# Stage boundaries of a two-layer decoder kernel, with the last two and the next four weight items done for one half of the sequence and then for the other

## The reference

```
c_act = silu(c)
for i in (0, 1):
    sh_m, sc_m, g_m, sh_f, sc_f, g_f = split(c_act @ mod_w[i] + mod_b[i], 6)
    h = modulate(rmsnorm(x, norm_mix_g[i]), sh_m, sc_m)
    y = gla_mixer(h, ...) if i == 0 else mla_attention(h, ..., shared_kv)
    x = x + (1 + g_m) * y
    h = modulate(rmsnorm(x, norm_ffn_g[i]), sh_f, sc_f)
    x = x + (1 + g_f) * conv_ffn(h, ...)      # up (2048 -> 2*5632), conv, silu, down
return rmsnorm(x, final_norm_g)
```

## Time and profile before

| | |
|---|---|
| Median of three runs | 2383.03 us (2381.65 to 2386.59) |
| The profiled execution, its own time | 2379.23 us |
| Its span | 2377.1 us |
| TensorE busy | 2301.8 us (97%) |
| VectorE busy | 1849.8 us (78%) |
| ScalarE busy | 1096.3 us (46%) |
| Mean granted TensorE clock | 0.986 |
| HBM over the span | 266 GB/s |

### The profile page before, as it was taken

The page is one execution under the profiler, slowest core; times in us unless marked ns, Lnnn a source line. Parts: engine busy times, 40 slices in busy tenths (PEclk is TensorE's granted clock), DMA queues, the critical chain, the costliest instruction groups (busy, mean ns, idle before and its releaser), DMA issues.

```text
span 2377.1 us, 26862 instructions
## 1 busy us (share of the span) xinstructions
PE 2301.8 (97%) x10800; PEld 1865.5 (78%) x10800; DVE 1849.8 (78%) x1766; ACT 1096.3 (46%) x1192; POOL 111.3 (5%) x127
## 2 busy tenths in 40 slices
PE   5999999999999999999998999999999999999997
PEld 2478887788887888878886888778887888878886
DVE  5868997888997898889898777787787556564565
ACT  2244443444554354533554545434654345544453
POOL 0021740000000000000000000000000000000000
PEclk8999999999999999999999999999999999999999
DMA  9957789788987998889888375785776555555554
GB/s 362 385 201 287 256 298 354 271 305 299 339 327 271 350 342 306 291 327 378 313 285 325 120 238 184 274 327 215 280 282 213 193 182 191 177 186 192 187 182 154
DMA packets 259807, 632.89 MB, mean 266 GB/s; under 512 B 23505, under 2 KB 32745, under 8 KB 233978
## 3 DMA queue, kind: packets, MB, share of 16 engines
q1 hardware_dynamic: 258050, 625.90, 74.1%
q10 hardware_dynamic: 1656, 5.60, 0.6%
HBM read 629.36 MB, written 2.10 MB: 266 GB/s over the span
## 4 chain that ended last, share of the span: by engine, by line
PE 49%; issue 34%; DVE 8%; DMA 5%; ACT 2%; SPq 1%; POOL 0%; POOLq 0%; DVEq 0%; ACTq 0%
PE gm L1960 12%; PE gm L1961 12%; PE gm L1967 12%; DVE acc L1242 2%; PE tp L2003 2%; DVE w_lo L1225 2%; DMA mods<-in_mod_w_dram 1%; PE gm L1952 1%; ACT w_hi L763 1%; PE gm L1954 1%; PE gm L1953 1%; PE ms L2113 1%; DMA raw<-in_ffn_w_down_dram 1%; PE ms L2247 1%; DMA raw<-in_mla_w_o_dram 1%
## 5 line engine op out<-in xcount | busy, mean ns | idle before, releaser
L1225 DVE TENSOR_TENSOR w_lo<-raw,w_hi 128x2048 fp32r<-128x2048 f32 (+1 forms) x378 | 851.9, 2255 | 325.3 <-ACT w_hi L763 323.6
L763 ACT ACTIVATE w_hi<-raw 128x2048 fp32r<-128x2048 f32 (+1 forms) x378 | 703.8, 1864 | 697.2 <-DMA raw<-in_ffn_w_up_dram 241.7
L1960 PE MATMUL gm<-w_hi,h_hi 128*128 128x512 f32 x1816 | 720.6, 397 | 1.7 <-DVE h_lo L1353 1.6
L1961 PE MATMUL gm<-w_hi,h_lo 128*128 128x512 f32 x1816 | 708.1, 390 | 0.0
L1967 PE MATMUL gm<-w_lo,h_hi 128*128 128x512 f32 x1816 | 448.7, 389 | 0.0
L1242 DVE SCALAR_TENSOR_TENSOR acc<-mods,c_col,acc 128x2048 f32<-128x2048 f32 x180 | 422.7, 2348 | 5.4 <-DMA mods<-in_mod_w_dram 4.2
L1960 PEld LDWEIGHTS gm<-w_hi,h_hi 128*128 128x128 f32 x1816 | 341.1, 188 | 78.0 <-issue 4.4
L1967 PEld LDWEIGHTS gm<-w_lo,h_hi 128*128 128x128 f32 x1816 | 340.8, 188 | 70.8
L1961 PEld LDWEIGHTS gm<-w_hi,h_lo 128*128 128x128 f32 x1816 | 341.3, 188 | 69.9 <-issue 1.7
L1960 PE MATMUL gm<-w_hi,a_hi 128*128 128x512 f32 x692 | 273.4, 395 | 11.1 <-DVE a_lo L1727 7.9
L1961 PE MATMUL gm<-w_hi,a_lo 128*128 128x512 f32 x692 | 269.6, 390 | 0.0
(11 more groups left out here) (275 smaller groups left out, 2137.5 us busy)
## 6 DMA issues: line engine op xcount, KB each, us to landing
raw<-in_ffn_w_up_dram SPq DMA_DIRECT2D x176, 1024.0 KB, 5.1
mods<-in_mod_w_dram SPq DMA_DIRECT2D x170, 1024.0 KB, 7.2
raw<-in_ffn_w_down_dram SPq DMA_DIRECT2D x64, 1024.0 KB, 5.1
raw<-in_gla_w_in_dram SPq DMA_DIRECT2D x48, 1024.0 KB, 5.2
mods<-in_kv_mod_w_dram SPq DMA_DIRECT2D x32, 1024.0 KB, 7.0
raw<-in_ffn_w_down_dram SPq DMA_DIRECT2D x32, 768.0 KB, 4.4
raw<-in_gla_w_o_dram SPq DMA_DIRECT2D x16, 1024.0 KB, 7.1
raw<-in_mla_w_o_dram SPq DMA_DIRECT2D x16, 1024.0 KB, 6.0
```

The source lines that it names most:

```text
L763: act.activation(w_hi[:, k % RAW, 0:words], raw[:, k % RAW, 0:words], ACT.Copy).then_inc(hi_made, 1)
L1225: dve.tensor_tensor(w_lo[:, k % RAW, 0:words], raw[:, k % RAW, 0:words], w_hi[:, k % RAW, 0:words].bitcast(F32), ALU.subtract).then_inc(lo ...
L1960: pe.matmul(o, hi_s[:, kt, tok], wh[:, j, :], start=kt == 0, stop=False)
L1961: pe.matmul(o, lo_s[:, kt, tok], wh[:, j, :], start=False, stop=False)
```

## The change

At each boundary the last two items of the stage and the first four of the next are done for t = 0 and then for t = 1. The normalised rows have a place per half: `x_tok[0]` over the second `mods` slot, `x_tok[1]` over `gate_b`. Fill f of a boundary is now four feature tiles of one token half: t = f // 4, tiles 4 (f % 4) to 4 (f % 4) + 3. Mean and power are made per half. The column sums come behind both last items, in two parts of eight columns. The first modulation load of `up00` and of `up10` waits for all eight fills. `add_last`, `boundary_root`, `normalise_chunks`, `first_split`, `reduced` and `late_normalise` go, the loops over items are otherwise as they were, `MOD_PLACES` too.

```diff
+    x_tok = (place("x_tok0", MD + 8192, [P, D], F32), place("x_tok1", GU, [P, D], F32))
...  # SP
+                elif n == first_mod("up00"):
+                    sp.wait_ge(tp_done, a["norm1"].tp + 8)
...  # ScalarE
+            def round_fill(name, f, dst):
+                act.wait_ge(both_made, 4 * BOUND[name] + f // 2 + 1)
+                act.activation(part(dst, f), both_v[:, :, :], ACT.Copy).then_inc(split_hi, 1)
+            def scale_fill(name, f, dst, scale, shift):
...
+                for j in range(4):        # 128 x 128 each, tp -> both_a
...
+                act.activation(part(dst, f), both_a[:, :, :], ACT.Copy).then_inc(split_hi, 1)
+            def turn_boundary(stage, name, nxt, dst, scale, shift, columns):
+                last_square(stage, name, 0)
+                normalise_rest(name, 0)       # 128 x 1536
+                last_square(stage, name, 1)
+                hi(nxt + 2)
+                round_fill(name, 0, dst)
+                act.wait_ge(columns_on, columns - (name != "norm2"))
+                scale_fill(name, 1, dst, scale, shift)
+                normalise_rest(name, 1)
+                round_fill(name, 2, dst)
+                act.wait_ge(columns_on, columns)
+                scale_fill(name, 3, dst, scale, shift)
+                hi(nxt + 3)
+                round_fill(name, 4, dst)
+                scale_fill(name, 5, dst, scale, shift)
+                round_fill(name, 6, dst)
+                scale_fill(name, 7, dst, scale, shift)
...  # VectorE
+            def add_half(stage, name, t):
+                if t == 0:
+                    dve.wait_ge(sq_made, 8 * BOUND[name] + 6)
...                    # the two sums of squares
+                    dve.wait_ge(half_used, BOUND[name] + 1)
...                    # product with the gate, sum into x, for t = 0
+                else:
+                    dve.wait_ge(item_used, a[stage].item + 16)
...                    # the same for t = 1
+                add_half(stage, name, 0)
+                mean_token(name, 0)
+                normalise_first(0)            # 128 x 512
+                lo(nxt + 1)
+                add_half(stage, name, 1)
+                mean_token(name, 1)
+                reduced_half(columns, 0)
+                scaled(0)                     # 4 of 128 x 128, tp -> both_v
+                low_part(0)
+                low_part(1)
+                normalise_first(1)
+                reduced_half(columns, 1)
+                scaled(2)
+                low_part(2)
+                lo(nxt + 2)
+                low_part(3)
+                scaled(4)
+                low_part(4)
+                lo(nxt + 3)
+                low_part(5)
+                scaled(6)
+                low_part(6)
+                low_part(7)
...  # TensorE
+            def last_items(stage, name, columns, specs, **how):
+                for t in range(TT):
+                    for i, spec in enumerate(specs):
+                        turns = t == 1 and i == 0 and name != "final"
+                        ins = token_item(t, *spec, middle=(lambda: token_fill(name, 0)) if turns else None, **how)
+                        if turns:
+                            token_fill(name, 1)
+                    if t == 0:
+                        ins.then_inc(half_used, 1)
+                if columns:
+                    reduce_mod(columns)
+            def first_items(name, first, fills, *src):
+                for t in range(TT):
+                    for k in range(4):
+                        f = 4 * t + k
+                        pe.wait_ge(tp_free, a[name].tp + f + 1)
+                        if f + 2 < fills:
+                            token_fill(name, f + 2)
+                        token_item(t, first + k, first + k, *src, 0, k)
```

More of the change, by code:

```diff
@@ L547, in load_item, with first_mod @@
                 sp.dma_start(dst, src).then_inc(raw_in[n % RAW], 16)
+            def first_mod(name):
+                return min(m[0] for item_, ms_ in mod_at.items() if item_ >= a[name].item for m in ms_)
             def load_mod(n, g, kt):
@@ L734, in _ @@
                 root(TT * h, TT, DV, o_sums, TT * (h + 1), o_rstd)
[L735 to L738, removed]
+            for name in ("norm1", "norm2"):
+                mean_root(name, 0)
+                mean_root(name, 1)
+            mean_root("norm3", 0, TT)
+            mean_root("norm4", 0, TT)
             pool.wait_ge(tp_free, at["norm4"].tp + 2)
@@ L828, in turn_boundary, with last_square @@
[L828 to L839, removed]
+            def last_square(stage, name, t):
+                if t == 0:
+                    act.wait_ge(x_half, BOUND[name] + 1)
+                else:
+                    act.wait_ge(x_added, added[stage] + 4)
+                chunk_squares(name, 3, t)
@@ L856, in turn_two @@
                 kv, mix = ab[:, A_OF["kv"]], ab[:, A_OF["mix1"]]
[L857 to L860, removed]
+                turn_boundary("down02", "norm2", next_item, a_hi, kv, ab[:, A_OF["kv"] + 1], COLUMNS_ON[9])
+                for f in range(8, 16):
+                    if f % 2:
                         hi(next_item + (f + 1) // 2)
@@ L2036, in reduce_mod @@
                 else:
[L2037 to L2041 removed]
+                    for half in range(2):
+                        o = ms_open(fill + half)
+                        for j in range(8):
+                            c0 = (8 * half + j) * P
+                            ins = pe.matmul(o[:, j:j + 1], acc[:, g % 2, c0:c0 + P], ones[:, 0:1],
+                                            start=True, stop=True)
+                        ins.then_inc(ms_done, 1)
             def reduce_turned(g, part):
@@ L2090, in body @@
                 def body(i, turned=None, last=False):
-                    for k in range(8):
+                    for k in range(8 - LAST[name] if last else 8):
                         if k % 4 == 0:
@@ L2094, in body @@
                         turn = turned if k < 4 else None
-                        item(s.item + 8 * i + k, s.item + k, hi_s, lo_s, k // 4, k % 4, turn=turn,
-                             halves=last and k == 7)
+                        item(s.item + 8 * i + k, s.item + k, hi_s, lo_s, k // 4, k % 4, turn=turn)
                         if turned and k >= 4:
@@ L2302, in _ @@
             section("gla_out", h_hi, h_lo, turn_o)
-            reduce_mod(4)
+            s = a["gla_out"]
+            last_items("gla_out", "norm1", 4, [(s.item + k, s.item + k, h_hi, h_lo, 1, k % 4) for k in range(16 - LAST["gla_out"], 16)])
             def turn_pair(layer, g, i, j):
@@ L2343, in ffn @@
                             gm_free(s.chunk + ch)
+                        if g == 2 and k >= 16 - LAST[name]:
+                            if k == 16 - LAST[name]:
+                                last_items(name, ("norm2", "final")[layer], (10, None)[layer],
+                                           [(s.item + n, s.item + n, a_hi, a_lo, 1, DOWN[2][n][1]) for n in range(k, 16)],
+                                           k_tiles=blocks, total=4 * blocks)
+                            continue
                         if ch == 0:
@@ L2359, in _ @@
             s, m = a["latent"], a["mla"]
-            reduce_mod(10)
-            for k in range(8):
-                if k % 4 == 0:
-                    gm_free(s.chunk + k // 4)
-                src = (a_hi, a_lo) if k < 4 else (h_hi, h_lo)
-                first = KT if k >= 4 else 0
-                item(s.item + k, s.item + k, *src, k // 4, k % 4,
-                     turn=lambda kt, first=first: turn_wide("norm2", first + kt, fills=16))
+            gm_free(s.chunk)
+            first_items("norm2", s.item, 16, a_hi, a_lo)
+            gm_free(s.chunk + 1)
+            for k in range(4, 8):
+                item(s.item + k, s.item + k, h_hi, h_lo, 1, k % 4,
+                     turn=lambda kt: turn_wide("norm2", KT + kt, x_tok, 16))
             def turn_latents(name, side):
```

397 lines of the change are left out of this document (193 added, 204 removed).

## The result

| | before | after |
|---|---|---|
| median of the runs (four each, on one chip) | 2383.60 us | 2405.53 us |
| lowest to highest | 2381.65 to 2386.59 | 2404.45 to 2410.68 |
| profiled execution: span | 2377.1 us | 2402.7 us |

The change makes the kernel slower: ratio 1.0092, 95% interval 1.0075 to 1.0108. The forecast was 2404 us.

A forecast was written before the change was run, and what follows sets the result against it. TensorE, busy 97%, bounds the kernel; at stage boundaries VectorE's backlog makes the sum late. Norm1 +9.0, norm5 +8.95, norm2 +8.1 and the end -2.5 sum to +23.5: 2402.7 or 2406.5 by base, stated 2404 us, range 2388 to 2413.

The forecast's parts named there:

- (a): Norm1, last two items: half 0 is signalled at 517.45, but busy VectorE starts its sum at 522.51, 5.06 us later.
- (b): Norm1, second pass: TensorE stands 7.7 us at fill 0's transposes, waiting for the normalised half 0; bounds 2.6 and 8.5.
- (c): Rest of norm1's second pass: low clock behind the wait, pass ends at 533.9, +11.0 us; 2.6 less at full rate.
- the rival of a clock that stays up: Boundaries: the 7.7 us of standing stay but 2.6 x 3 go, 2396 us; chance 0.08.
- (d): Norm1, pass's end to next stage's first matmul: half 1's chain takes 6.9 us against 8.62, -1.7; column sums cost nothing.
- (e): Next four items after norm1: one transpose group fewer, -0.5, low clock longer, +0.2, together -0.3 us; bound +1.7.
- (f): End of the kernel: half 0's output leaves early, last transfer issued at about 2369.5 instead of 2371.51; -2.5 us, bounds -1 and -4.
- (g): SP's load queue: weight slots come free later, but item 4 is there 1.6 us early; cost 0, bound +2.2 each.
- The rival on the other side: Boundaries: VectorE takes the half at its signal, stall 2.6 us with the clock up, -0.4 each, 2379.3 us; chance 0.07.

The follow-up runs named there:

- e5: Kernel of e2 with ScalarE's rounding of the next stage's second item also moved behind the normalisation of half 0: 2397.79 us, ratio 1.0070.
- e2: Changed kernel with VectorE's w_lo and, at norm1 and norm5, a modulation product moved behind half 0's normalisation; at norm2 two products go earlier: 2403.74 us, 1.0076.
- e6: Changed kernel with 26 further matmuls that nobody reads ahead of fill 0's transposes in the second pass: 2398.54 us, ratio 1.0061.
- e7: Changed kernel with column sums moved into the second pass's stall, and half 0's first two parts made ahead of the sum of half 1: 2383.16 us, 1.0003.
- e4: Kernel before with only the end as in the changed kernel, the three stage boundaries as before: 2380.26 us, ratio 0.9980.
- e10: Kernel before with the new end and the third group's item order in the down projections' first two groups: 2367.23 us, ratio 0.9915.
- e11: Kernel before, unchanged, profiled a second time: 2380.85 us, span 2379.0.
- e12: Changed kernel with column sums in the stall, w_lo and w_hi behind the half, and e10's item order: 2372.58 us, ratio 0.9942.

## Why the prediction was right, by its steps

**(a) held.** VectorE's sum of half 0 started at 522.09 against 522.51, and half 0's signal lay for 5 us, as forecast. e5 shows that the queues are the cause: with their work behind the half the stall is 3 us. But the prediction saw only one of two queues. It named VectorE, and priced the rival as if VectorE were all; e2 freed VectorE at norm1 and gained 0.7 us of stall; with ScalarE's queue freed too (e5) another 3.0 us went.

**(b) held, the size was off.** 6.75 us of standing at norm1 for 7.7 forecast: from the sum's start to the transposes 3.76 us, not 4.47. The single-token power took 0.55 instead of 0.69 us, and the step of 0.38 for the sums of squares came ahead of the sum's start. At norm2 it was 6.13 where the same sum gives 7.9, at norm5 5.11 for 7.35. At norm5 the sum came 8.8 us behind S where it had been 10.2; what made VectorE less late was not tried. From S to G the three boundaries came to +10.2, +8.7 and +7.8 us, for +11.0, +10.1 and +10.65.

**(c) held to 0.1 us at norm1.** From the resumed transposes to G 6.88 us, forecast 6.92 (at norm5 6.17 for the same 6.92); e6 puts the clock's part at 2.2, 2.4 and 1.6, forecast 2.6. The row 525 to 530 of the changed kernel shows 0.50, the lower of the two levels, so the rival of a clock that stays up is out. The Trainium skill (TensorE: Matmul & The Clock Gate, on HAM oscillation) says that a long wait between bursts of matmuls does this; by that rule, the trace agrees, with 0.50 behind 6.75 us.

**(d) held.** G to F 6.72, 6.50 and 6.71 us, forecast 6.9; four scalings 1.37 us on VectorE and 1.49 on ScalarE, forecast 1.4. e7 shows what the forecast passed over: all but 0.35 us of these are order alone, since half 0 doesn't need what it is queued behind.

**(e)** +0.4 at norm1, -0.2 and -0.1, forecast -0.3 each. The group of transposes that it took at half a us is 0.35 us at the full clock (538.04 to 538.40 in the trace of before).

**(f) too small.** -3.8 us, forecast -2.5, within its bound; e4 confirms it. The issue of the last transfer moved by 2.2 us against S, forecast 2.0. The rest is the tail from that issue to the end of the span, 4.0 us where it was 5.6, for which the sum allowed 0.5. The power of each half took 0.54 us there, with the product ahead of the mean, and not the 1.61 us of before: as the prediction had read it.

**(g) was the step that failed.** It priced the late slots at nothing, because the first load had time enough. It had: no weight was late within the four items. The cost came 55 us later, 1.45 us behind norm1, where weights and modulation take the DMA engines' whole time. The check was made at the next transfer and not at the end of the stretch in which the DMA engines are full. In the latent stage, items 4 to 7 took 1.1 us more; in the profiles with norm2 by halves it is 0.6 (e6) to 1.6 us, in e4, e10 and e11 nothing. So it belongs to the change, but its cause was not tried.

**The sum hides this.** The boundaries came to +21.3 us where +26.0 were forecast, the end to -3.8 for -2.5, and the rest to +8.1 for 0. About 4.5 of the 8.1 are the clock, which fell behind three ordinary stalls in the profile of after and behind none in that of before; 1.45 and 1.1 are the costs under (g). At the start of the second down projection TensorE waits 1.5 us more for VectorE, which was not tried; gains of under 1 us elsewhere make up the sum. Without the three falls the spans differ by 21.1 us, the medians by 21.9. Such falls come without the change too, in four of fifteen cases with the old boundaries (before, e4, e11) and in 23 of 45 with halves; whether the change makes them more frequent is not shown. So it is in part luck that 2404 lies so near to 2405.5: the boundaries and the end came 6.0 us below their forecast, and 8.1 us that the forecast didn't have took their place.

The prediction also had two bases, the profile (2402.7) and the median (2406.5), and chose between them without a cause for their difference. That the profile of before has no fall of the clock is one: e11 has two, and a span 1.9 us longer. It isn't all, since e11 too lies below the other runs on its chip.

**The rival on the other side** (VectorE takes the half at its signal, 2379.3) was wrong in its price too. e5 has that stall, and norm1 and norm5 lie 5.0 and 3.6 us above before from S to F, where the price was 1.1 us (+3.2 for the pass, -2.1 behind it). At norm1 the pass took +6.9 us, since the clock was low behind 3 us. At norm5 the clock stayed up and the pass took +3.4, as priced, but the stretch behind it didn't get shorter (+0.1), since the work moved behind half 0 made VectorE late for half 1.

## What to carry to other kernels

When work is split so that a second engine can start sooner, look at every engine of the chain for what is queued ahead of the early half, and move all of it at once; one freed queue shows only the next. Whatever TensorE must do anyway and does not need the awaited result (here the column sums) belongs into the wait, and work for the first half ahead of the sum of the second: that was worth 22 us here (e7), the split of the boundaries itself nothing (e12 is 5 us above e10). Work that is moved out of the way must also not be in the way of the second half (e5 at norm5). And look for the unremarkable stalls of 2 us elsewhere first: an item order changed in one line gained 13 us by the medians and 15 by the ratios (e10 against e4).

## What the runs showed of the hardware

A stall of 1.9 to 2.7 us may or may not bring the clock down. Over the twelve profiles that have the five ordinary stalls (0.3 to 3.1 us, in the first two down projections, the latent attention's heads, its output projection and the fifth down projection), a 5 us stretch at or behind the stall shows a clock below 0.97 in 27 of 60 cases. Length alone doesn't decide it: at the first down projection 1.93 and 2.08 us were followed by it, 2.49 and 2.66 us were not. One such fall costs about 1.5 us (1.6 at 747.70, 1.4 at 1568.62), and none followed the stall of 1.20 us at 1818. With up to five such falls in one execution (e7's profile) this can be one source of the spread of several us between executions of one kernel; that it is wasn't shown, since each kernel but the one before has a single profile.

The power of one column of 128 took 0.55 us on GpSimd where two columns took 0.69, and 1.61 at the end of the kernel before, where VectorE had started a product of two tensors in SBUF 0.2 us earlier (2367.52, 1.22 us).

The clock can fall during the 32 matmuls with one output column, without a wait ahead of them: at norm1 of the kernel before they follow the 512-wide ones directly and take 4.61 us, where they take 3.63 at norm2; the mean clock from 525 to 530 is 0.53.
